# The down stage's last round in two parts, with four token tiles of the final norm between the second part's products

## The chip, the cores and the metric

The kernel runs on one core of a Trainium2 chip, as one launch. The metric is the device time of one execution in microseconds (us); lower is better. TensorE (PE) multiplies, VectorE (DVE), ScalarE (ACT) and GpSimd (POOL) do the rest, and SyncE (SP) issues the DMAs. Each engine runs its own instructions in program order; between engines, order comes from semaphore waits alone.

## What is computed

One layer of a streaming encoder for 1024 prompt tokens and 128 sample tokens (8 requests of 16), all in float32, width 1024:

```python
xp = half_ffn(xp, ...)            # f1:  x + 0.5 * ((silu(a) * b) @ w_down),  a, b = split(rmsnorm(x) @ w_up)
h  = rmsnorm(x);  x = x + W_out(gates * (sparse attention, matrix memory))
xp = half_ffn(xp, ...)            # f2
y  = rmsnorm(x) * norm_final      # the final norm
```

`w_up` is 1024 x 5632 and `w_down` 2816 x 1024. The outputs are y for all tokens, new keys and values, and the new memory states. The change touches both FFNs and the final norm; the middle of the layer is left as it is.

## The kernel before

`ffn` (from line 520) is built twice, as f1 and f2. The 1152 tokens are held transposed in `xT`, eight row blocks of 128 features by 1152 tokens, in two halves of 576. Each matrix product is done by a scheme of seven block products instead of eight: a weight tile of 256 columns is split into 2 x 2 blocks, the activations into 2 x 2 (feature halves and token halves), sums and differences are formed of both, and products 0 to 6 of each tile go through PSUM chains that yield four output blocks. Block 0 and 2 belong to the first token half, blocks 1 and 3 to the second. Each number is carried as a high and a low part, so a product of weights and activations is three matmuls (`product3`, lines 517 to 519) for each of two token quarters and each feature group.

The up stage has weight tiles 0 to 21, the down stage tiles 22 to 41 in five rounds of four tiles: four rounds over two groups of hidden features (12 matmuls a product) and the last one over three groups (18 matmuls a product). The hidden activations are packed by ScalarE and VectorE (`pack_hi`, `pack_lo`, after `combine`) into one of three staging buffers, stored to DRAM by SyncE, and loaded again as operands of the down rounds (`load_operand`).

The order is written out by hand. `AT` lists all products; `step(n, q)` is the place of product q of tile n in it. At each step TensorE waits for the low part of its weights (`lo_ok`) and for its PSUM bank (`free_bank`, line 1072), and does the product. ScalarE casts the weights of four products later (`split_hi`, line 751), GpSimd subtracts for the low part (line 869). VectorE first evicts the product just done (`accumulate`, lines 923 and 927: half of the chain is added to a block of `xT`), and then does the rest that tables place at this step: `pack_lo` (line 972) from `LO_AT`, `combine` (lines 960 to 968) from `COMB_AT`, weight terms (differences of weight blocks, line 890) from `TERMS_AT`, the residual (`ADD_AT`), and in f1 additions of squares (line 981). VectorE and ScalarE stay in this order whatever comes late.

Two lines decide which products depend on each other:

```python
CHAIN = (0, 1, 0, 2, 0, 2, 0)          # PSUM chain of products 0..6
def bank(n, q): return (n - 2 + CHAIN[q]) % 3
```

Products 0, 2, 4, 6 of a tile follow each other in one bank pair, 3 and 5 in another, 1 alone. Product q may begin only when the bank's former product has been evicted. In the order 0 to 6 there is always another product between two of the same bank.

The final norm (`FinalNorm`) comes after the last product and its eviction, for nine tiles of 128 tokens: `turn` (eight transposes on TensorE into a PSUM pair, line 482), `square` with the row's sum (ScalarE, 491), `inverse` (VectorE, 498 and 501), `root` (ScalarE, 505), `result` (VectorE, 511), and the store (SyncE, 474). Tiles 0 to 7 alternate between two PSUM pairs, tile 8 has a third. Turn t waits for result t − 2.

Of the kernel before, what the change touches and what calls it, by code (L numbers as in the profile page):

```python
# [24 lines left out]
P = 128  # L25
# [422 lines left out]
class FinalNorm:  # L448
# [12 lines left out]
    def pair(self, t):  # L461
        at = 4 if t == 8 else t % 2 * 2
        return self.ps[:, at:at + 2, :].rearrange("p b n -> p (b n)")
# [5 lines left out]
    def store(self, sp):  # L469
        for t in range(NT):  # L470
            sp.wait_ge(self.r_ok, t + 1)
            dst = self.out["y_prompt"][0, t * P:(t + 1) * P, :] if t < NTP else \
                self.out["y_sample"].rearrange("b q d -> (b q) d")
            sp.dma_start(dst, self.res[:, t]).then_inc(self.st, 16)
        sp.wait_ge(self.st, 16 * NT)

    def turn(self, pe, t):

        if 2 <= t < 8:
            pe.wait_ge(self.r_ok, t - 1)  # L480
# [26 lines left out]
    def result(self, dve, t):  # L507

        dve.wait_ge(self.root_ok, t + 1)
        dve.wait_ge(self.ld, 16)  # L510
        self.nc.vector.scalar_tensor_tensor(self.res[:, t], self.pair(t), self.K["root"][:, t:t + 1],  # L511
                                            self.gain[:], ALU.mult, ALU.mult).then_inc(self.r_ok, 1)
# [9 lines left out]
def ffn(nc, ctx, M, K, w_up, w_down, gain, xT, xT_at, places, h_dram, r_dram, tag, first, last_io=None):  # L522
# [9 lines left out]
    def step(n, q):  # L532
        return 8 * n + q if n < 2 else 16 + 7 * (n - 2) + q

    def slot_no(n, x):
        return 4 * n + x if n < 2 else 8 + 7 * (n - 2) + x
# [3 lines left out]

    SLOTS, STEPS = slot_no(UPS + DOWNS, 0), step(UPS + DOWNS, 0)
    U_SLOTS, U_STEPS = slot_no(UPS, 0), step(UPS, 0)
    AT = [(n, q) for n in range(UPS + DOWNS) for q in range(8 if n < 2 else 7)]
    OWNER = [(n, x) for n in range(UPS + DOWNS) for x in range(4 if n < 2 else 7)]
    FREED = {last_use(j - RING): j for j in range(RING, SLOTS)}
    TERMS_AT = {}
    for n in range(2, UPS + DOWNS):
        late = n == UPS
        for i, e in enumerate((-4, -4, 0 if late else -3, 1 if late else -1)):
            TERMS_AT.setdefault(step(n, 0) + e, []).append((n, i))  # L550
    HI_AT, LO_AT, COMB_AT = {}, {}, {}
    for g in range(NG):
        b = step(2, 0) - 7 if g == 0 else step(2 * g + 1, 0)
        for i, e in enumerate((8, 9, 10, 10, 11, 12, 13) if g == 0 else (2, 5, 6, 8, 9, 10, 11)):
            HI_AT.setdefault(b + e, []).append((g, i))
            LO_AT.setdefault(b + e + 1, []).append((g, i))
        COMB_AT[b + (9 if g == 0 else 7)] = (g, 0)
        COMB_AT[b + (11 if g == 0 else 8)] = (g, 1)
    SUM_HI_AT = {step(0, 7) + e: e for e in range(8)}
    RAW_AT = {step(n, 0) - (10 if n > 2 else 12): n for n in range(2, UPS + DOWNS)}  # L560
    assert len(RAW_AT) == UPS + DOWNS - 2
    SQ_STEP = (1, 4, 5, 6)
# [10 lines left out]
    for r in range(len(ROUNDS)):  # L573
        for q in range(7):
            at, size = OPERAND[r, q]
            s = max(u[2] for u in used if u[0] < at + size and at < u[0] + u[1])
            LOAD_AT.setdefault(max(s + 1, step(UPS + 4 * r - 4, 3 * q)) if r else s + 1, []).append((r, q, s + 1))
            used.append((at, size, step(UPS + 4 * r + 3, q)))
# [4 lines left out]
    with ExitStack() as mem, M.scope():  # L583
# [33 lines left out]
        if last_io is not None:  # L617
            z = FinalNorm(nc, sem, K, xT, *last_io, M.at("z_gain", [P, D_MODEL], K["acc_at"]),
                          M.at("z_junk", [P, D_MODEL], main_at), M.at("z_res", [P, NT, D_MODEL], main_at + 4 * D_MODEL), ps)
# [3 lines left out]
        def round_of(n):  # L623
            return ROUNDS[(n - UPS) // 4]
# [56 lines left out]
        def y_block(m, i):  # L681
            k, t = 2 * (m % 4) + (0, 1, 1, 0)[i], (0, 1, 0, 1)[i]
            return xT[:, k, t * HT:(t + 1) * HT]

        with nc.Block() as block:
            @block.sync
            def _(sp):
# [4 lines left out]
                def load_raw(n):  # L692
                    sp.wait_ge(lo_ok, slot_no(n - 1, 0))
# [44 lines left out]
                if last_io is not None:  # L738
                    z.load(sp)
# [3 lines left out]
            def _(act):  # L743
                def split_hi(j):
                    n, x = OWNER[j]
                    weights_in(act, n)
                    if n >= 2 and isinstance(SOURCE[x], int):
                        act.wait_ge(t_ok, 4 * (n - 2) + SOURCE[x] + 1)
# [61 lines left out]
                def square(e):  # L810
                    m, i = DOWNS - 4 + e // 4, e % 4
                    act.wait_ge(dn_ev, 7 * m + SQ_STEP[i] + 1)
                    if e >= 4:
                        act.wait_ge(sum_ok, e - 3)
                    else:
                        act.wait_ge(pl_ok, 7 * NG)
                    t = (0, 1, 0, 1)[i]
                    dst = K["acc"][:, t * HT:(t + 1) * HT] if e < 2 else sq[e % 2][:]
                    nc.scalar.activation(dst, y_block(m, i), ACT.Square).then_inc(sq_ok, 1)

                def rest(n, q):
                    s = step(n, q)
# [10 lines left out]
                    if last_io is None and n >= UPS + DOWNS - 4:  # L833
                        m = n - (UPS + DOWNS - 4)
                        if m and q == 0:
                            square(4 * m - 1)
                        if q in (2, 5, 6):
                            square(4 * m + (2, 5, 6).index(q))
# [21 lines left out]
                else:  # L860
                    for t in range(NT):
# [10 lines left out]
            def _(dve):  # L872
                v = nc.vector

                def weight_term(n, i):
                    weights_in(dve, n)
                    count = 4 * (n - 2) + i
                    if n > 2:
                        dve.wait_ge(lo_ok, slot_no(n - 1, TERM_SLOT[i]) + 1)
                    else:  # L880
                        dve.wait_ge(norm.sl_ok, 2)
                    if n == UPS and i >= 2:
# [3 lines left out]
                    if i in (1, 3):  # L886
                        dve.wait_ge(t_ok, count if i == 1 else count - 1)
                    a, b = ((part(n, 0, 1), part(n, 0, 0)), (part(n, 1, 1), term(n, 0)), (part(n, 1, 1), part(n, 0, 1)),
                            (part(n, 1, 0), term(n, 1)))[i]
# [18 lines left out]
                def accumulate(n, q):  # L908
                    m = n - UPS
                    i = (0, 0, 2, 1, 1, 2, 3)[q]  # L910
                    before = 7 * m + {1: 1, 4: 4, 5: 3}[q] if q in (1, 4, 5) else \
                        7 * (m - 4) + {0: 2, 2: 6, 3: 5, 6: 7}[q]
                    dve.wait_ge(mm_ok, step(n, q) + 1)
# [7 lines left out]
                    y = pairs(y_block(m, i))  # L921
                    if m < 4 and q in (0, 2, 3, 6):
                        v.tensor_scalar(y, chain(n, q), 0.5, None, ALU.mult).then_inc(dn_ev, 1)
                        return
                    if before > 0:
                        dve.wait_ge(dn_ev, before)
                    v.scalar_tensor_tensor(y, chain(n, q), 0.5, y, ALU.mult, ALU.add).then_inc(dn_ev, 1)  # L927
# [20 lines left out]
                def add_residual(e, t):  # L948
                    k, tok = 2 * (e % 4) + e // 4, norm.tok(t)
                    dve.wait_ge(y_in[e % 2], 16 * (e // 2 + 1))  # L950
                    dve.wait_ge(dn_ev, 7 * (4 + e + 1))
# [23 lines left out]
                def add_square(e):  # L975
                    t = (0, 1, 0, 1)[e % 4]
                    a = K["acc"][:, t * HT:(t + 1) * HT]
                    dve.wait_ge(sq_ok, e + 1)
                    if e >= 4:
                        dve.wait_ge(sum_ok, e - 3)  # L980
                    v.tensor_tensor(a, a, sq[e % 2][:], ALU.add).then_inc(sum_ok, 1)

                def rest(n, q):
                    s = step(n, q)
# [10 lines left out]
                    if last_io is None and n >= UPS + DOWNS - 4:  # L995
                        m = n - (UPS + DOWNS - 4)
                        if m and q < 2:
                            add_square(4 * m - 2 + q)
                        if m and q in (3, 6):
                            add_square(4 * m + (3, 6).index(q))  # L1000
# [32 lines left out]
                else:  # L1033
                    for t in range(NT):
# [4 lines left out]
            def _(pe):  # L1039
# [32 lines left out]
                def free_bank(n, q):  # L1072
                    m, adds = n - UPS, 3 * (n - 2)
                    if q == 0:
                        if n == 2:
                            pe.wait_ge(hm_ok, 3)
                        elif m <= 0:
                            pe.wait_ge(ad_ok, adds - 2)
                        else:
                            pe.wait_ge(dn_ev, 7 * (m - 1) + 2)  # L1080
                    if q == 1:
                        if n == 2:
                            pe.wait_ge(hm_ok, 4)
                        elif m <= 0:
                            pe.wait_ge(ad_ok, adds)
                        else:
                            pe.wait_ge(dn_ev, 7 * (m - 1) + 6)
                    if q == 3:
                        if m > 0:
                            pe.wait_ge(dn_ev, 7 * m)  # L1090
                        elif n % 2:
# [3 lines left out]
                    if q in (2, 4, 5, 6):  # L1095
                        if m >= 0:
                            pe.wait_ge(dn_ev, 7 * m + {2: 1, 4: 3, 5: 4, 6: 5}[q])
                        elif q == 6:
                            pe.wait_ge(ad_ok, adds + 2)
                        else:  # L1100
                            pe.wait_ge(cp_ok, adds + {2: 1, 4: 2, 5: 3}[q])
# [9 lines left out]
                def down(n, q):  # L1111
                    j, r = slot_no(n, q), (n - UPS) // 4
# [4 lines left out]
                    products(chain(n, q), j, lambda k: xd[r, q][:, k, 0], lambda k: xd[r, q][:, k, 1], len(ROUNDS[r]),  # L1117
                             q in (0, 1, 3))
# [12 lines left out]
                if last_io is not None:  # L1131
                    pe.wait_ge(dn_ev, 7 * DOWNS)
                    for t in range(NT):
# [2050 lines left out]
```

## Time and profile before

| | us |
|---|---|
| median of 3 runs | 2536.09 (2535.38 to 2536.65) |
| the profiled execution | 2538.52 |
| its span | 2536.7 |
| TensorE busy | 2469.3 |
| VectorE busy | 1651.9 |
| ScalarE busy | 992.5 |
| GpSimd busy | 914.1 |
| mean DMA rate | 142 GB/s |

All comes from one execution recorded by the hardware profiler. Busy time counts an engine's own instructions; TensorE's weight loads (PEld) run beside its matmuls. A matmul's end is modelled, so matmuls overlap in the record; the distance of their starts is the pace. "Idle before <- X" is the time an engine stood before an instruction, and X is what ended it, inferred from semaphores. f1 runs from about 80 us to 780 us, the middle until about 1750 us, f2 from there to the end. f1's down stage begins at about 528 us and f2's at about 2257 us; f2's last round of products ends at 2508.8 us.

### The profile page before, as it was taken

To read this page: it belongs to the slowest core of one execution; us is meant where nothing else is said; L and a number is where in the kernel's file an instruction comes from. 1 tells how busy PE (TensorE), PEld (TensorE's weight loads), DVE (VectorE), ACT (ScalarE), POOL (GpSimd) and SP (SyncE) were. 2 spreads that over 40 slices of the span, in tenths; PEclk is the share of its full clock that TensorE was granted. 3 is DMA by queue.
4 is the path that set the end of the run, shared out by engine and by line. 5 is a ranking of instruction groups with operands and counts; after the bars stand their busy time and mean duration, and the time that the engine had idled before them with its cause. 6 is when DMAs were issued, how large, how long until landed. Compare 5 with 4: busy or idle time off the path is not lost. (4 is left out here: it accounts for less than half of the span.)

```text
span 2536.7 us, 43065 instructions
## 1 busy us (share of the span) xinstructions
PE 2469.3 (97%) x16970; PEld 2399.8 (95%) x16970; DVE 1651.9 (65%) x2570; ACT 992.5 (39%) x1875; POOL 914.1 (36%) x739
## 2 busy tenths in 40 slices
PE   7999999999998999999998999998999999999997
PEld 7999999999997989999997888998999999999997
DVE  8776766667765328998645653424867576667864
ACT  5444444422233332212557864323434344432223
POOL 1444444444455111212224103421344444444442
PEclk8999999999998999999998999998999999999998
DMA  5343343497634212112334422333234334487751
GB/s 211 114 149 131 140 149 136 152 360 280 261 133 142 64 54 79 52 52 85 100 90 100 60 58 89 126 108 125 89 136 161 127 136 144 144 320 287 292 190 75
DMA packets 227304, 361.47 MB, mean 142 GB/s; under 512 B 39644, under 2 KB 174872, under 8 KB 226720
## 3 DMA queue, kind: packets, MB, share of 16 engines
q1 hardware_dynamic: 227104, 358.72, 41.0%
q8 instruction: 135, 2.21, 0.4%
q14 instruction: 65, 0.53, 0.1%
HBM read 231.21 MB, written 126.26 MB: 141 GB/s over the span
## 5 line engine op out<-in xcount | busy, mean ns | idle before, releaser
L517 PE MATMUL f1ps<-f1xs_lo,f1w_hi 128*128 128x288 f32 x1248 | 369.0, 296 | 3.7 <-DVE f1xs_lo L417 3.7
L517 PE MATMUL f2ps<-f2xs_lo,f2w_hi 128*128 128x288 f32 x1248 | 368.3, 295 | 3.7 <-DVE f2xs_lo L417 3.7
L519 PE MATMUL f1ps<-f1xs_hi,f1w_hi 128*128 128x288 f32 x1248 | 369.2, 296 | 0.0
L519 PE MATMUL f2ps<-f2xs_hi,f2w_hi 128*128 128x288 f32 x1248 | 368.7, 295 | 0.0
L518 PE MATMUL f1ps<-f1xs_hi,f1w_lo 128*128 128x288 f32 x1248 | 368.6, 295 | 0.0
L518 PE MATMUL f2ps<-f2xs_hi,f2w_lo 128*128 128x288 f32 x1248 | 368.1, 295 | 0.0
L517 PE MATMUL d_ps<-xn_lo,d_w_hi 128*128 128x384 f32 x864 | 298.5, 345 | 6.9 <-POOL xn_lo L297 5.3
L518 PE MATMUL d_ps<-xn_hi,d_w_lo 128*128 128x384 f32 x864 | 293.6, 340 | 0.0
L519 PE MATMUL d_ps<-xn_hi,d_w_hi 128*128 128x384 f32 x864 | 293.5, 340 | 0.0
L517 PEld LDWEIGHTS f1ps<-f1xs_lo,f1w_hi 128*128 128x128 f32 x1248 | 235.1, 188 | 5.1 <-POOL f1w_lo L869 4.1
L517 PEld LDWEIGHTS f2ps<-f2xs_lo,f2w_hi 128*128 128x128 f32 x1248 | 234.7, 188 | 4.7 <-issue 3.9
L518 PEld LDWEIGHTS f1ps<-f1xs_hi,f1w_lo 128*128 128x128 f32 x1248 | 235.1, 188 | 0.1
L519 PEld LDWEIGHTS f1ps<-f1xs_hi,f1w_hi 128*128 128x128 f32 x1248 | 235.2, 188 | 0.0
L519 PEld LDWEIGHTS f2ps<-f2xs_hi,f2w_hi 128*128 128x128 f32 x1248 | 234.8, 188 | 0.0
L518 PEld LDWEIGHTS f2ps<-f2xs_hi,f2w_lo 128*128 128x128 f32 x1248 | 234.7, 188 | 0.1
L1565 POOL TENSOR_TENSOR d_w_lo<-d_raw,d_w_hi 128x1024 fp32r<-128x1024 f32 x36 | 86.4, 2399 | 406.6 <-ACT d_w_hi L1430 406.6
L517 PE MATMUL f1ps<-f1xd,f1dw_hi 128*128 128x288 f32 x616 | 182.7, 297 | 3.4 <-issue 2.8
L517 PE MATMUL f2ps<-f2xd,f2dw_hi 128*128 128x288 f32 x616 | 183.1, 297 | 3.0 <-issue 2.8
L1859 DVE TENSOR_SCALAR_CACHE_REDUCE sel_hits<-DM,sel_cand 128x1024 uint8<-128x1024 f32 (+6 forms) x217 | 184.9, 917 | 1.1
L519 PE MATMUL f2ps<-f2xd,f2dw_hi 128*128 128x288 f32 x616 | 183.2, 297 | 0.0
L518 PE MATMUL f2ps<-f2xd,f2dw_lo 128*128 128x288 f32 x616 | 182.7, 297 | 0.0
L519 PE MATMUL f1ps<-f1xd,f1dw_hi 128*128 128x288 f32 x616 | 182.6, 296 | 0.0
(416 smaller groups left out, 6069.1 us busy)
## 6 DMA issues: line engine op xcount, KB each, us to landing
h_dram<-f1stg SPq DMA_DIRECT2D x77, 576.0 KB, 3.3
f1xd<-h_dram SPq DMA_DIRECT2D x77, 576.0 KB, 8.0
h_dram<-f2stg SPq DMA_DIRECT2D x77, 576.0 KB, 3.3
f2xd<-h_dram SPq DMA_DIRECT2D x77, 576.0 KB, 8.1
f1raw<-in_w_ffn_up SPq DMA_DIRECT2D x22, 1024.0 KB, 6.4
f2raw<-in_w_ffn_up SPq DMA_DIRECT2D x22, 1024.0 KB, 6.4
d_raw<-in_w_in SPq DMA_DIRECT2D x35, 512.0 KB, 5.1
p_dram<-stage SPq DMA_DIRECT2D x24, 576.0 KB, 3.4
```

The costliest lines, as they stand in the source:

```text
L517: nc.tensor.matmul(out, w_hi, x_lo, start=first, stop=False, skip_group_check=onto)
L518: nc.tensor.matmul(out, w_lo, x_hi, start=False, stop=False, skip_group_check=onto)
L519: return nc.tensor.matmul(out, w_hi, x_hi, start=False, stop=final, skip_group_check=onto)
L1565: nc.gpsimd.tensor_tensor(w_lo[:, n0 % 2], raw[:, n0 % 2], w_hi[:, n0 % 2].bitcast(F32), ALU.subtract).then_inc(lo_ok, 1)
L1859: v.tensor_scalar(hits[:, off:off + L], views[j], limit, None, ALU.is_ge, ALU.add, accum_out=cnt[:, j:j + 1]).then_inc(cnt_ok, 1)
```

## The change

- The last round's four tiles become eight. Tiles 38 to 41 do products 0, 1, 2, 3 and 5 and so finish blocks 0 and 2, the first 576 tokens. Tiles 42 to 45 do products 4 and 6, which add to blocks 1 and 3. This holds for f1 and f2.
- Product 2 of the first part is evicted into three blocks (2, 3, 1) instead of one, since the chain is cut there. Tiles 42 to 45 load their weights again (768 KB each) and form three weight terms each; tiles 38 to 41 form two instead of four.
- The second part's chains use banks 2 and 3 in turn, products 4 and 6 of a tile in the same bank.
- `free_bank` now finds the bank's former product in `AT` and waits for the last of its evictions.
- In f2, TensorE turns token tiles 0 to 3 ahead of the second, third, fifth and sixth product of the second part; ScalarE's square and root and VectorE's inverse follow at that step, the result at the next. Tiles 4 to 8 remain behind the last product and use four PSUM pairs. In f1 the squares are reordered to the blocks as they are finished.
- The packing and combining of the last up group (g = 10) moves: from steps 2, 5, 6, 8, 9, 10, 11 after the start of tile 21 to 8, 9, 10, 10, 11, 12, 13, the combines from 7 and 8 to 9 and 11; step 7 is the first product of the down stage.
- The final norm's gain is loaded after the last residual, its buffers lie elsewhere.

```diff
+    TILES = UPS + DOWNS + 4
+    SPLIT, LATE = TILES - 8, TILES - 4
+    PRODUCTS = [tuple(range(8))] * 2 + [tuple(range(7))] * (SPLIT - 2) + [(0, 1, 2, 3, 5)] * 4 + [(4, 6)] * 4
+        if n >= LATE:
+            places_of = (0, -4), (2, -4), (3, -3)
+        elif n >= SPLIT:
+            places_of = (0, -4), (1, -4)
+    ONTO = [((0,), (0,), (2,), (1,), (1,), (2,), (3,)), {0: (0,), 1: (0,), 2: (2, 3, 1), 3: (1,), 5: (2,)}, {4: (1,), 6: (3,)}]
...
-        for i, e in enumerate((8, 9, 10, 10, 11, 12, 13) if g == 0 else (2, 5, 6, 8, 9, 10, 11)):
+        late = g in (0, NG - 1)
+        for i, e in enumerate((8, 9, 10, 10, 11, 12, 13) if late else (2, 5, 6, 8, 9, 10, 11)):
...
+        COMB_AT[b + (9 if late else 7)] = (g, 0)
+        COMB_AT[b + (11 if late else 8)] = (g, 1)
...
+    TURN_AT = {step(LATE, x): t for t, x in enumerate((1, 2, 4, 5))} if last_io is not None else {}
...
         def bank(n, q):
+            if n >= LATE:
+                return 2 + n % 2
             return (n - 2 + CHAIN[q]) % 3
...
                 def free_bank(n, q):
+                    before = [x for x in AT[AT.index((2, 0)):AT.index((n, q))] if bank(*x) == bank(n, q)]
+                    if before and before[-1][0] >= UPS:
+                        pe.wait_ge(dn_ev, events_to(*before[-1]))
+                    elif n >= LATE:
+                        return
...
+                    if at(n, q) in TURN_AT:
+                        pe.wait_ge(dn_ev, events_to(LATE - 1, 5))
+                        z.turn(pe, TURN_AT[at(n, q)])
...
-                    for t in range(NT):
+                    for t in range(4, NT):
                         z.turn(pe, t)
```

In `FinalNorm` the pair of tile t becomes `2 * (t % 2 if t < 4 else t % 4)`, and turn t waits for result t − 2 up to tile 5, for the result of tile 3 at tiles 6 and 7, and for that of tile 4 at tile 8.

## Rows read from the trace of the kernel before

**Rows 1.** The page, busy time of each engine.
```profile
PE 2469.3 (97%) x16970; PEld 2399.8 (95%) x16970; DVE 1651.9 (65%) x2570; ACT 992.5 (39%) x1875; POOL 914.1 (36%) x739
```
**Rows 2.** Windows, last round: us, busy PE PEld DVE ACT POOL, PEclk, DMA, GB/s.
```profile
2475.00:2509.00 34.00, 33.80 (x256) 33.57 (x254) 14.53 (x20) 5.80 (x11) 12.44 (x11) 1.00 0.00 1
```
**Rows 3.** Timeline, TensorE, end of the last round: start, duration, instruction, idle before.
```profile
2508.52 0.29 PE L519 MATMUL f2ps<-f2xd,f2dw_hi 128*128 128x288 f32 x1
2509.66 1.97 PE L482 MATMUL f2ps<-ident_sb,xT 128*128 128x128 f32 x16 [0.85 <-DVE xT L927]
```
**Rows 4.** Timeline, VectorE, the last two evictions.
```profile
2506.47 0.76 DVE L927 SCALAR_TENSOR_TENSOR xT<-f2ps,xT 128x576 f32<-128x576 f32 x1 [1.62 <-PE f2ps L519]
2508.84 0.76 DVE L927 SCALAR_TENSOR_TENSOR xT<-f2ps,xT 128x576 f32<-128x576 f32 x1 [1.62 <-PE f2ps L519]
```
**Rows 5.** The chain that ended last, in the tail: start, us, what.
```profile
2509.66 1.10 PE f2ps L482 x8
2510.78 1.11 ACT z_junk L491 x2
...
2513.45 1.30 DVE z_res L511
...
2516.79 1.12 ACT z_junk L491 x2
...
2518.56 1.28 DVE z_res L511
...
2520.38 1.30 DVE z_res L511
...
2532.42 1.28 DVE z_res L511
```
**Rows 6.** Timeline, VectorE, f2's last round: an eviction and two weight terms.
```profile
2468.39 0.76 DVE L927 SCALAR_TENSOR_TENSOR xT<-f2ps,xT 128x576 f32<-128x576 f32 x1 [1.62 <-PE f2ps L519]
2469.07 0.55 DVE L890 TENSOR_TENSOR f2dts<-f2draw 128x384 f32<-128x384 f32 x1
2469.75 1.16 DVE L890 TENSOR_TENSOR f2dts<-f2draw,f2dts 128x384 f32<-128x384 f32 x1
```
**Rows 7.** Timeline, VectorE, f1's last round: additions of squares.
```profile
741.20 0.75 DVE L981 TENSOR_TENSOR acc<-acc,f1sq 128x576 f32<-128x576 f32 x1
...
747.04 1.57 DVE L981 TENSOR_TENSOR acc<-acc,f1sq 128x576 f32<-128x576 f32 x1
```
**Rows 8.** Timeline, VectorE, eviction of product 2 of tile 22.
```profile
2265.51 0.74 DVE L923 TENSOR_SCALAR xT<-f2ps 128x576 f32<-128x576 f32 x1
```
**Rows 9.** Timeline, TensorE, first down tile of f2.
```profile
2263.29 0.29 PE L519 MATMUL f2ps<-f2xd,f2dw_hi 128*128 128x288 f32 x1
2266.36 0.58 PE L517 MATMUL f2ps<-f2xd,f2dw_hi 128*128 128x288 f32 x1 [2.78 <-issue]
...
2272.01 0.44 PE L519 MATMUL f2ps<-f2xd,f2dw_hi 128*128 128x288 f32 x1
2272.26 0.38 PE L517 MATMUL f2ps<-f2xd,f2dw_hi 128*128 128x288 f32 x1
```
**Rows 10.** Windows of TensorE: us, busy, PEclk, DMA, GB/s.
```profile
806.00:808.00 2.00, 1.27 (x7) 1.00 1.20 299
...
2265.00:2270.00 5.00, 3.64 (x15) 0.56 1.03 422
```
**Rows 11.** DMA issues: out<-in, count, KB each, median us to landing.
```profile
h_dram<-f2stg SPq DMA_DIRECT2D x77, 576.0 KB, 3.3
...
f2draw<-in_w_ffn_down SPq DMA_DIRECT2D x4, 768.0 KB, 5.0
...
z_gain<-in_norm_final SPq DMA_DIRECT2D x1, 512.0 KB, 5.6
```
**Rows 12.** Waits (2255 to 2280; TensorE's 795 to 860): total, times, longest.
```profile
ACT f2stg L808 <- DMA h_dram<-f2stg: 3.3, 3, 2.4
...
PE d_ps L517 <- POOL xn_lo L297: 2.3, 5, 0.5
```

More of the change, by code:

```diff
@@ L530, in ffn @@
     CHAIN = (0, 1, 0, 2, 0, 2, 0)
[L532 to L536, printed above, removed]
+    TILES = UPS + DOWNS + 4
+    SPLIT, LATE = TILES - 8, TILES - 4
+    PRODUCTS = [tuple(range(8))] * 2 + [tuple(range(7))] * (SPLIT - 2) + [(0, 1, 2, 3, 5)] * 4 + [(4, 6)] * 4
+    STEP0 = [sum(len(x) for x in PRODUCTS[:n]) for n in range(TILES + 1)]
+    SLOT0 = [4 * n if n < 2 else STEP0[n] - 8 for n in range(TILES + 1)]
@@ L538, in last_use, with step, at, slot_no @@
+    def step(n, x):
+        return STEP0[n] + x
+    def at(n, q):
+        return STEP0[n] + PRODUCTS[n].index(q)
+    def slot_no(n, q):
+        return 4 * n + q if n < 2 else at(n, q) - 8
     def last_use(j):
         return 8 * (j // 4) + 4 + j % 4 if j < 8 else j + 8
[L541 to L544, printed above, removed]
+    SLOTS, STEPS = SLOT0[TILES], STEP0[TILES]
@@ L545, in ffn @@
+    U_SLOTS, U_STEPS = SLOT0[UPS], STEP0[UPS]
+    AT = [(n, q) for n in range(TILES) for q in PRODUCTS[n]]
+    OWNER = [(n, x) for n in range(TILES) for x in (range(4) if n < 2 else PRODUCTS[n])]
     FREED = {last_use(j - RING): j for j in range(RING, SLOTS)}
[L546 to L550, printed above, removed]
+    TERMS, TERMS_AT = [], {}
@@ L551, in ffn, with events_to, touched_before @@
+    EVENTS = [(n, q, i) for n in range(UPS, TILES) for q in PRODUCTS[n]
+              for i in ONTO[0 if n < SPLIT else 1 if n < LATE else 2][q]]
+    def events_to(n, q):
+        return 1 + max(x for x, e in enumerate(EVENTS) if e[:2] == (n, q))
+    def touched_before(x):
+        n, q, i = EVENTS[x]
+        return max([y + 1 for y in range(x) if (EVENTS[y][0] - n) % 4 == 0 and EVENTS[y][2] == i], default=0)
     HI_AT, LO_AT, COMB_AT = {}, {}, {}
@@ L623, in round_of @@
         def round_of(n):
-            return ROUNDS[(n - UPS) // 4]
+            return ROUNDS[min((n - UPS) // 4, len(ROUNDS) - 1)]
         def raw_of(n):
@@ L832, in rest @@
                         pack_hi(g, i)
[L833 to L838, printed above, removed]
+                    if last_io is None:
+                        for e in SQ_AT.get(s, ()):
+                            square(e)
+                    if s in TURN_AT:
+                        z.square(act, TURN_AT[s])
+                        z.root(act, TURN_AT[s])
                 norm.root(act)
@@ L920, in accumulate @@
                         dve.wait_ge(ra_ok, 2 * (m - 7))
[L921 to L927, printed above, removed]
+                    for x, (tile, product, i) in enumerate(EVENTS):
+                        if (tile, product) != (n, q):
+                            continue
+                        y = pairs(y_block(n, i))
+                        if touched_before(x) == 0:
+                            v.tensor_scalar(y, chain(n, q), 0.5, None, ALU.mult).then_inc(dn_ev, 1)
+                        else:
+                            dve.wait_ge(dn_ev, touched_before(x))
+                            v.scalar_tensor_tensor(y, chain(n, q), 0.5, y, ALU.mult, ALU.add).then_inc(dn_ev, 1)
                 def evict(n, q):
@@ L994, in rest @@
                         add_residual(*ADD_AT[s])
[L995 to L1000, printed above, removed]
+                    if last_io is None:
+                        for e in SUM_AT.get(s, ()):
+                            if e % 8:
+                                add_square(e)
+                    if s - 1 in TURN_AT:
+                        z.result(dve, TURN_AT[s - 1])
+                    if s in TURN_AT:
+                        z.inverse(dve, TURN_AT[s])
                 norm.inverse(dve)
@@ L1033, in _ @@
                 else:
-                    for t in range(NT):
+                    for t in range(4, NT):
                         z.inverse(dve, t)
@@ L1131, in _ @@
                 if last_io is not None:
-                    pe.wait_ge(dn_ev, 7 * DOWNS)
-                    for t in range(NT):
+                    pe.wait_ge(dn_ev, len(EVENTS))
+                    for t in range(4, NT):
                         z.turn(pe, t)
```

140 lines of the change are left out of this document (73 added, 67 removed).

## The prediction

> **What bounds the kernel now.** I read the page's busy times first: TensorE is busy 97% of the span [rows 1], so any time comes from its idle stretches, from work it does beside the products, or from the tail after its last product. The timelines come next, cut to the end. In the last down round TensorE is busy 33.80 of 34.00 us at full clock while the DMA stands still [rows 2], and VectorE evicts one product every 2.37 us [rows 4]: 18 matmuls each, so 0.132 us a matmul, and 12 matmuls or 1.58 us in the rounds of two groups. No product waits there, because the one ahead of it never touches the same bank. After the last eviction come nine token tiles of the final norm, in two bank pairs; the span ends at 2536.7 us, 27.1 us after that eviction's end at 2509.60. One more loss lies where the down stage begins: TensorE stands still for 2.78 us, and its matmuls then come 0.25 us apart until 2272.26 [rows 9].
>
> The trace is of f2, the second FFN; f1 runs the same code without the final norm and with squares instead.
>
> **The price of a product that follows its own bank.** The last eviction is the pattern: final matmul starts 2508.52 and lasts 0.29, VectorE starts 2508.84, takes 0.76, and TensorE starts again at 2509.66 [rows 3, 4]. Without a wait the next matmul would have started at 2508.65. So an adjacent dependence costs 1.0 us, and I take 1.05, since the first matmul after a wait is longer (0.58 against 0.44 in [rows 9]). Bounds: 0.85 (eviction and its two hand-overs, if the rest is hidden by the queue) and 1.3.
>
> **First part (tiles of products 0, 1, 2, 3, 5).** Products 3 and 5 share a bank and used to have product 4 between them. Now they are adjacent, and product 5 waits for the eviction of 3. That is four stalls in each FFN. Ahead of that eviction VectorE has product 2's evictions, now three instead of one: two at the spacing of back-to-back work, 0.68, and one of 0.76 [rows 4, 6], 2.1 us, which fits into 2.38. In f2 the two weight terms after product 1 take 0.55 and 1.16 [rows 6]; with the eviction that is 2.5 us, 0.15 over, still absorbed. In the fourth tile a third term (0.55 to 1.16 [rows 6], taken 0.7) follows the three evictions and delays the one of product 3 by 0.45. f2: 4 × 1.05 + 0.45 = 4.65 us. In f1 an addition of squares (0.75, or 1.57 beside a busy GpSimd [rows 7]) also stands behind the terms from the second tile on: 0.68 + 0.55 + 1.16 + 0.75 = 3.15 to 3.4, so the three evictions end about 0.7 after product 3 does. With 0.55 more in each of three tiles and 0.7 more in the last: 4.2 + 1.65 + 0.7 = 6.5 us.
>
> **Second part (tiles of products 4, 6).** Both use one bank, and only 6 continues the sum of 4, so each 6 waits for the eviction of 4. The first 4 uses the bank of the product just ahead of it too. f1: 5 stalls. VectorE there has, per tile, two evictions, three terms and two additions of squares, 6.5 us against 4.76 + 1.05 of TensorE, so it has no slack; 5 × 1.1 = 5.5 us. f1 loses 12.0 us together, and its own tail stays.
>
> f2: the first 4 stalls (1.05). Four turns of eight transposes go between the products: the first took 1.10 and two of them 1.97 [rows 3, 5], so 4 × 1.05, 4.2 us (3.9 to 4.4). Those ahead of a product 6 (two of them) cover the eviction. The two products 6 without one stall, and here the norm's small work gets into VectorE's queue. Behind its eviction at each turn stands the wait for ScalarE's square (1.11 [rows 5]), which itself stands behind a weight cast, which waits for a weight term on VectorE. I followed the queues from the end of the first product 6 (time 0): term and cast 2.2, square until 3.5, inverse until 3.85. The next product 4 ends at 3.5, its eviction therefore ends at 4.6, and product 6 starts at 4.65 (1.25 stalled). The result of tile 0 (1.30 [rows 5]) must wait for two more terms, 7.6; the third turn needs its bank pair and stalls 0.6. The fourth turn waits 0.2 for the result of tile 1, and the last product 6 stalls 0.85. Together 2.9 us of waits, with the first 4's 1.05 and the turns 8.2 us. The second reading of the weights costs nothing: its load takes 5.0 us [rows 11] and starts three products, 7.1 us, ahead of the terms; uncovered it would hold VectorE some 2 us a tile. The gain row likewise: 5.6 us [rows 11], some 15 us ahead. f2 loses 4.65 + 8.2 = 12.9 us before its tail.
>
> **The tail.** Now it holds five tiles with four bank pairs. From the last eviction's end: turn 1.10, square 1.11, inverse and root 0.65 (from 2516.79 + 1.12 to 2518.56), result 1.30 [rows 5]. Then each further tile costs what two results lie apart when their turn is ready, 20.38 − 18.56 = 1.82 [rows 5]: 4 × 1.82 = 7.3. After the last result 3.0 for the store (2536.7 − 2533.7, [rows 5]). Sum 14.5 us. The first root waits for its function table: 1.56 us lie between its square's end and the first result (2513.45 − 2511.89) where later tiles have 0.65 [rows 5]; that moves ahead, beside products. Gain 27.1 − 14.5 = 12.6 us; bounds 11.5 (one more wait for a turn) and 13.5. So f2's part nets 0.3 us slower: what the tail gives, the stalls and the turns take.
>
> **The last up group's packing moves about one down tile later.** In the old order VectorE does packing and combining in front of the eviction of product 2 of the first down tile: it starts at 2265.51 [rows 8], though product 3 behind it had ended at 2263.58 and so product 2 by 2262.0. TensorE waits for it, 2266.36 − 2263.29 less one matmul, 2.9 us, and then runs 24 matmuls at 0.25 instead of 0.13, 2.7 us more [rows 9]; the granted clock was 0.56 there, near its lower level of 1.2 GHz [rows 10]. This loss is 5.6 us per FFN. The new order frees this eviction and piles the packing up afterwards. In 11 products of 1.58 us, 17.4 us, VectorE has eleven evictions, seven packings, four combines and six terms, 28 pieces at about 0.7, 19.6 us. By my walk down the queues product 5 waits 0.4, product 6 waits 1.1 (behind a packing and two terms), product 1 of the next tile 1.5 (behind two packings, two combines, a term), product 2 of it 2.2, for ScalarE's packing must wait until a store has left its staging buffer: 3.3 us when the DMA is free [rows 11], up to 7 when full; ScalarE waited up to 2.4 for it before [rows 12]. Sum 5.2 us, and 1 us more for some matmuls at the lower clock. Per FFN that is 6.2 against the old 5.6, so +0.6; bounds −5.6 (all gone) and +5 (full DMA and a second clock drop).
>
> **Sum.** f1 12.0, f2 12.9 − 12.6 = 0.3, packing 2 × 0.6 = 1.2: +13.5 us. The profiled execution took 2538.5 us, its span 2536.7; by this it becomes 2552.0, span 2550.2. It lies 2.4 us over the median of the three runs, 2536.1; on that the forecast is 2549.6, taken as 2550.
>
> **Weighed against a rule.** In f1's second part TensorE would be busy 2.38 of 3.45 us, 69%, five times over. Rows show the clock at 1.00 in a stretch where it was busy 1.27 of 2.00 us, between waits of up to 0.5 us [rows 10, 12], and at half only after 2.78 us of standing [rows 9]. The Trainium skill's page "TensorE: Matmul & The Clock Gate", section "A second HAM failure mode: psum-queue depth-cycling", speaks against this change: matmul groups that pause briefly each time they cycle through PSUM banks can make the clock swing. By the row the sum stays +13.5; the rule's case is rival B, and nothing above uses it.
>
> **Rivals.**
> A, the forecast: stalls at 1 us, clock kept in the last round, 2550; own range 2543 to 2557. Chance 0.60.
> B, the clock falls in the last round. Place: the pauses of the parts, worst in f1's second. A matmul at the lower clock costs 0.12 more [rows 9], a product of 18 costs 2.1: over f1's eight late products 17 us, over half of them 8. 2558 to 2567, say 2562. For it: short repeated stalls that the old round lacks. Against: [rows 10]. 0.13.
> C, the other side: not slower. Place: the start of the down stage. If stores return in 3.3 us and no eviction queues, all 5.6 us in each FFN go: 12.3 − 11.2 = +1.1, 2537. It decides from about 4 us of gain per FFN (12.3 − 8 is inside the 5 us of no change), and each 0.2 us off the 16 stalls adds 3.2, to 2534. For it: evictions 0 to 3 are really freed. Against: VectorE's 20 us of work in 17.4. 0.15, of which a third lies below −0.2%.
> D, the change doesn't do what it says: the four early tiles come too late, because the weight loads of the second part or the norm's waits hold VectorE at each of the late tiles by some 2 us; 6 to 8 us more, 2557. 0.12.
>
> **Numbers.** 0.2% is 5 us, about what this kernel's measurement tells from none. Slower: A, B, D, and a little of C's upper end lies in no change: 0.82. Same 0.12, from C and the low end of A. Faster 0.06. The range 2539 to 2562 leaves out most of C and the upper part of B.
>
> **What would show it.** Product 5 of tiles 38 to 41 idle 0.85 us "<-DVE xT", in f1 up to 1.6; product 6 of the late tiles the same, five in f1. Span from last eviction to end near 14.5 us. Product 2 of the first down tile without a wait, and waits of 1 to 2 us in the tile after. Wrong if adjacent products wait under 0.5 us, if the down stage's start loses under 2 us, or if the granted clock falls in the last round.

## The result and the profile after

| | before | after |
|---|---|---|
| median | 2536.37 us (2535.38 to 2538.38, 4 runs) | 2563.84 us (2560.88 to 2565.94, 4 runs) |
| profiled execution / its span | 2538.52 / 2536.7 | 2560.88 / 2559.1 |

The ratio is 1.0106, 95% interval [1.0091, 1.0121]: the changed kernel is 1.1% slower. The direction was as forecast (2550 us), the size was not, and it lies 2 us above the range's upper end of 2562.

The page's busy times of the kernel after, to be held against [rows 1], come first. TensorE's work has not grown: it is busy 1.6 us less than before in a span 22.4 us longer, so its added time is standing. VectorE's has grown by 7.4 us.

```profile
PE 2467.7 (96%) x16970; PEld 2395.3 (94%) x16970; DVE 1659.3 (65%) x2594; ACT 990.4 (39%) x1875; POOL 905.6 (35%) x739
```

To find where, I cut the two traces at marks that both have: the last up product's multiply on VectorE, the eviction of product 0 of tile 24 (two tiles into the down stage), the start of the last eviction, and the end of the span.

| us, from the timelines | before f1 | after f1 | before f2 | after f2 |
|---|---|---|---|---|
| start: last multiply to product 0 of tile 24 | 29.2 | 35.2 | 29.6 | 36.1 |
| rest: from there to the last eviction | 221.9 | 233.5 | 221.9 | 234.7 |
| tail: last eviction's end to the span's end | | | 27.1 | 14.5 |

The last round and the tail are as forecast: +11.6 and +12.8 us in the rest (forecast 12.0 and 12.9), 14.5 us of tail (forecast 14.5). The start costs 6.0 and 6.5 us more; forecast was 0.6.

**The last round.** VectorE's timeline in the first part of f2 (start, duration, instruction, idle before). The eviction after three in a row is product 3's, the next one product 5's. Their distance is 3.52 us, where undisturbed products lie 2.39 apart: a stall of 1.13.

```profile
2472.00 2.07 DVE L970 SCALAR_TENSOR_TENSOR xT<-f2ps,xT 128x576 f32<-128x576 f32 x3
2474.32 0.76 DVE L970 SCALAR_TENSOR_TENSOR xT<-f2ps,xT 128x576 f32<-128x576 f32 x1 [0.24 <-PE f2ps L519]
2477.84 0.76 DVE L970 SCALAR_TENSOR_TENSOR xT<-f2ps,xT 128x576 f32<-128x576 f32 x1 [2.76 <-PE f2ps L519]
```

The same place in f1, where an addition of squares stands ahead of the three evictions. Four evictions run together without a gap, so product 3's comes late and TensorE waits 1.47 us before 755.12.

```profile
751.37 0.74 DVE L1024 TENSOR_TENSOR acc<-acc,f1sq 128x576 f32<-128x576 f32 x1
752.04 2.93 DVE L970 SCALAR_TENSOR_TENSOR xT<-f1ps,xT 128x576 f32<-128x576 f32 x4
```
```profile
755.12 0.37 PE L517 MATMUL f1ps<-f1xd,f1dw_hi 128*128 128x288 f32 x1 [1.47 <-DVE xT L970]
```

The windows of the two last rounds show what became of the clock (us, busy PE PEld DVE ACT POOL with counts, PEclk, DMA, GB/s): TensorE pauses in 13 to 16% of the time, in pauses of 0.9 to 1.5 us, and the granted clock stays at 1.00.

```profile
740.00:760.00 20.00, 17.06 (x128) 16.86 (x128) 11.33 (x15) 4.83 (x9) 7.52 (x7) 1.00 0.14 41
760.00:790.00 30.00, 25.29 (x184) 24.28 (x184) 18.71 (x30) 9.43 (x17) 9.41 (x9) 1.00 0.25 79
```
```profile
2500.00:2545.00 45.00, 39.30 (x291) 37.64 (x290) 24.99 (x42) 11.88 (x24) 11.43 (x11) 1.00 0.31 112
```

The tail, the chain that ended last (start, us, what): the first result begins 0.65 us after its square's end, where [rows 5] had 1.56, so the function table's wait is out of the tail as forecast. The five results lie 1.81 apart.

```profile
2544.64 1.10 PE f2ps L482 x8
2545.74 0.02 issue
2545.76 1.12 ACT z_junk L491 x2
...
2547.53 1.28 DVE z_res L511
...
2549.34 1.28 DVE z_res L511
...
2554.78 1.28 DVE z_res L511
```

**The start of the down stage.** Here is the difference to the forecast. First the waits of the kernel after in f2, 2273 to 2312 us (engine, line, waited for what: us in total, times, longest). Follow the wait back: product 2 of tile 23 waits 5.7 us for an eviction (L967); VectorE waits 3.9 us for ScalarE's packing (L845); and ScalarE waits up to 6.7 us for a store to leave its staging buffer (the first line). Before, the line of that last wait read 3.3 us in 3 waits, the longest 2.4 [rows 12].

```profile
ACT f2stg L845 <- DMA h_dram<-f2stg: 11.9, 4, 6.7
...
PE f2ps L517 <- DVE xT L967: 5.7, 1, 5.7
DVE xT L967 <- PE f2ps L519: 5.7, 5, 2.0
...
DVE f2stg L1015 <- ACT f2stg L845: 3.9, 1, 3.9
PE f2ps L517 <- issue: 1.8, 2, 1.4
PE f2ps L517 <- DVE xT L970: 1.5, 1, 1.5
```

The timelines put them in order. SyncE's queue: ahead of the store issued at 2285.27 stand two loads of the next round's operands (L746, 576 KB each) and one of weights.

```profile
2283.42 1.27 SPq L746 DMA_DIRECT2D f2xd<-h_dram  x2
2284.73 0.49 SPq L736 DMA_DIRECT2D f2draw<-in_w_ffn_down  x1
2285.27 0.51 SPq L760 DMA_DIRECT2D h_dram<-f2stg  x1
```

The times from issue to landing of the seven stores between 2275 and 2300 us are spread as follows; the median over all 77 of this kernel is 3.3.

```profile
DMA to landing us min/median/max: 3.2/6.6/8.8
```

A slow return is not new at this place. In the kernel before, the six stores between 2258 and 2275 us were no quicker:

```profile
DMA to landing us min/median/max: 5.3/7.3/8.3
```

What the new order took away is the room for it. There are three staging buffers, so each packing takes the buffer of the third one before it. In the old order (steps 2, 5, 6, 8, 9, 10, 11) the last four packings come 6, 4, 4 and 3 steps after the one whose buffer they take; in the new (8, 9, 10, 10, 11, 12, 13) 2, 2, 2 and 3. ScalarE now waits at all four: 3.1 and 1.8 us for stores that took 3.7 and 3.2, then 6.7 for one that took 8.5, then 0.4.

ScalarE stands for that buffer from 2287.24 (2293.90 − 6.66) and gets it 8.6 us after the store's issue. Queued behind the packing on ScalarE is a weight cast.

```profile
2293.90 0.68 ACT L845 ACTIVATE f2stg<-f2g 128x576 fp32r<-128x576 f32 x1 [6.66 <-DMA h_dram<-f2stg]
2294.49 0.40 ACT L788 ACTIVATE f2dw_hi<-f2dts 128x256 fp32r<-128x256 f32 x1
```

VectorE stands at the low half of the same packing; the eviction that frees product 2's bank is two places behind it.

```profile
2294.61 0.76 DVE L1015 TENSOR_TENSOR f2stg<-f2g,f2stg 128x576 fp32r<-128x576 f32 x1 [3.94 <-ACT f2stg L845]
2295.29 0.95 DVE L934 TENSOR_TENSOR f2dts<-f2draw,f2dts 128x256 f32<-128x256 f32 x1
2296.16 0.74 DVE L967 TENSOR_SCALAR xT<-f2ps 128x576 f32<-128x576 f32 x1
```

TensorE starts again 0.89 us later, after 5.74 us, and its matmuls come 0.24 us apart until 2301.75. The windows show the granted clock: 1.00 in the first, 0.71 in the second, which holds most of the standing, 0.61 in the third, toward the lower level of 1.2 GHz.

```profile
2297.05 0.58 PE L517 MATMUL f2ps<-f2xd,f2dw_hi 128*128 128x288 f32 x1 [5.74 <-DVE xT L967]
2297.43 0.44 PE L518 MATMUL f2ps<-f2xd,f2dw_lo 128*128 128x288 f32 x1
2297.67 0.44 PE L519 MATMUL f2ps<-f2xd,f2dw_hi 128*128 128x288 f32 x1
```
```profile
2288.00:2293.00 5.00, 1.83 (x12) 1.62 (x12) 2.67 (x4) 0.00 (x0) 0.39 (x1) 1.00 1.00 313
2293.00:2298.00 5.00, 0.95 (x4) 0.98 (x5) 3.39 (x5) 2.28 (x5) 2.64 (x3) 0.71 0.88 333
2298.00:2303.00 5.00, 5.00 (x26) 5.00 (x25) 1.41 (x3) 0.66 (x2) 1.01 (x2) 0.61 0.96 294
```

Waits of 5.7 + 1.8 + 1.5 us and 20 matmuls 0.11 late each (2.1) make 11.1 us, against 2.8 + 2.7 before: 5.6 of the 6.5 that the start grew. The idle time in front of a matmul is less than the wait costs, and there are now four waits for one. Counted from start to start of the 184 matmuls (those 0.16 to 0.32 us apart as slow ones, more than that as standing, each above the pace of 0.132), it is 10.0 us of standing against 3.2 and 2.3 us of slow matmuls against 2.6 in f2, 9.7 against 3.6 and 1.6 against 1.8 in f1. All the growth is standing; the lower clock is in both kernels, and has no part in it. In f1 the longest wait is 5.5 us and ends on product 2's weights (the cast queued behind the same waiting packing) instead of its bank.

### The profile page after: what moved, and what is told of

The parts are those of the page before. It is cut to its first block and busy times, and to the rows that moved or that the text cites. A ratio compares the mean times of both kernels' runs of the same rounds, so it can differ in the third digit from the quotient of the medians.

```text
span 2559.1 us, 43105 instructions
## 1 busy us (share of the span) xinstructions
PE 2467.7 (96%) x16970; PEld 2395.3 (94%) x16970; DVE 1659.3 (65%) x2594; ACT 990.4 (39%) x1875; POOL 905.6 (35%) x739
## 5 line engine op out<-in xcount | busy, mean ns | idle before, releaser
L518 PEld LDWEIGHTS f2ps<-f2xs_hi,f2w_lo 128*128 128x128 f32 x1248 | 234.7, 188 | 0.1
```

Of the source, the lines that this page charges most:

```text
L518: nc.tensor.matmul(out, w_lo, x_hi, start=False, stop=False, skip_group_check=onto)
```

## The experiments

Theory: the late packing costs about 6 us per FFN, because ScalarE now waits for staging buffers whose stores come back late behind the next round's loads; the stalls and turns of the last round cost what was forecast. Rivals: the packing's cost is VectorE's order of work alone; it is of the memory layout or of some other part of the change; or the parts don't add up. Each run below was timed against the kernel before on the same chip; its median there was 2536.75 to 2537.38 us. "Start", "rest" and "tail" are the segments of the table above, f1 and f2.

**pack_back**: the change without its packing edit.

```diff
-        late = g in (0, NG - 1)
+        late = g == 0
```

> The changed kernel with the packing and combining of the last up group put back to its old steps; all else as changed. Theory: the later packing alone costs 6.0 us in f1 and 6.5 us in f2 over the old start of the down stage (time from the last up product's multiply to the eviction of product 0 of tile 24: 35.2 and 36.1 us against 29.2 and 29.6), so both return to 29.2 to 29.6 and the median falls from 2563.8 by 12 to 15 us, to 2549 to 2552. Rival: the start is slower for another part of the change (bank waits, order of the DMA issues), then it stays at 35 to 36 us and 2563.

Measured 2550.17 us (2548.24 to 2552.62, 5 runs), ratio 1.0053 [1.0040, 1.0067]. Start 29.3 and 29.2, rest 233.6 and 234.7, tail 14.5. So without the packing edit the change costs 13.4 us by the ratio, with it 26.9.

**pack_only**: the kernel before with the packing edit alone (the same line, the other way).

> The kernel before with only the later packing and combining of the last up group, in both FFNs. Theory: 2536.4 + 12.5, 2548 to 2552, with ScalarE waiting over 5 us for a staging buffer's store at the start of each down stage and TensorE standing 5 us behind it. Rival: without the split it makes no difference, 2535 to 2539.

Measured 2550.22 us (2548.10 to 2550.53, 5 runs), ratio 1.0051 [1.0038, 1.0063]. Start 35.7 and 35.7, rest 221.9 twice, tail 27.1. Alone it costs 12.9 us; 12.9 and 13.4 add up to the 26.9 within their intervals. The packing edit is half of the loss, and neither half needs the other.

**loads_later**: the change, with the loads of the down stage's second round issued at steps 10 to 25 of the stage instead of 0 to 18, each 7 to 10 steps later. (What was written down ahead of mid_loads and loads_only calls the same edit 10 to 15 steps later, in the last up group.)

```diff
-            LOAD_AT.setdefault(max(s + 1, step(UPS + 4 * r - 4, 3 * q)) if r else s + 1, []).append((r, q, s + 1))
+            first_at = step(UPS, 10 + 5 * q // 2) if r == 1 else step(UPS + 4 * r - 4, 3 * q)
+            LOAD_AT.setdefault(max(s + 1, first_at) if r else s + 1, []).append((r, q, s + 1))
```

> The changed kernel with the loads of the second round's operands issued from step 10 after the start of tile 22 on, one every two or three steps, instead of from step 0 every three. Theory: the store that ScalarE waits 6.7 us for is slow because those loads are ahead of it in the DMA queues; the wait falls under 4 us and the time by 4 to 8 us, 2556 to 2560. Rival: it is VectorE's load of work alone (19.6 us of pieces in 17.4), and the start stays at 35 to 36 us, 2562 to 2565.

Measured 2551.91 us (2546.66 to 2556.51, 4 runs), ratio 1.0057 [1.0042, 1.0073]: a gain of 12 us where 4 to 8 were expected, the same as pack_back, while all packing stays late. Start 29.5 twice, rest as in the change. Its waits in f2's start, 2265 to 2304 us, answer to those above: the longest for a store is 2.7 and TensorE's longest 2.5.

```profile
ACT f2stg L846 <- DMA h_dram<-f2stg: 7.6, 4, 2.7
...
PE f2ps L517 <- DVE xT L968: 2.5, 1, 2.5
PE f2ps L517 <- issue: 1.4, 1, 1.4
```

The DMA issues from 2270 to 2305 us (tile, engine, count, KB each, median us from issue to landing) say why; the first two rows are of the change, the last of this kernel. The store takes 6.6 us in the one and 4.0 in the other.

```profile
f2xd<-h_dram SPq DMA_DIRECT2D x10, 576.0 KB, 8.2
h_dram<-f2stg SPq DMA_DIRECT2D x7, 576.0 KB, 6.6
```
```profile
h_dram<-f2stg SPq DMA_DIRECT2D x7, 576.0 KB, 4.0
```

And the clock, in the windows over the wait and behind it, stayed at 1.00:

```profile
2280.00:2285.00 5.00, 2.17 (x15) 1.72 (x13) 4.34 (x7) 2.29 (x5) 2.08 (x3) 1.00 0.94 381
2285.00:2290.00 5.00, 4.95 (x37) 4.98 (x38) 3.71 (x5) 0.84 (x2) 2.86 (x4) 1.00 0.82 277
```

What the late packing costs over the old order is thus what its stores have to wait behind loads. It takes both, the short room between packings and the slow return: the old order with the same loads starts in 29.2 and 29.6 us, and the late order with those loads moved back in 29.5, against 35.2 and 36.1 for both together.

**order_swap**: the first part's tiles do product 3 before product 2, so that product 2 stands between 3 and 5, which share a bank.

```diff
-[(0, 1, 2, 3, 5)] * 4
+[(0, 1, 3, 2, 5)] * 4
```

> The changed kernel with products 2 and 3 of the first part's tiles exchanged (order 0, 1, 3, 2, 5), so that product 2 stands between 3 and 5, which share a bank. Theory: the four stalls in each FFN go, with what stood ahead of product 3's eviction: 4.65 us in f2 and 6.5 us in f1, so 11 us, 2551 to 2555, and no wait over 0.3 us before product 5. Rival: VectorE's three evictions and squares are what holds TensorE in f1, and the waits move to the product after; then 6 to 8 us, 2556 to 2558.

Measured 2553.77 us (2552.89 to 2557.58, 5 runs), ratio 1.0069 [1.0056, 1.0082]. Rest 229.0 and 230.5, 4.5 us less in f1 and 4.2 in f2. No wait over 0.2 us is left in the first part, but the rival is right in part: a wait has moved on. The first product of the second part, whose bank is that of the product just ahead of it, now waits 2.13 us in f1 and 1.46 in f2 (0.90 in both before the swap), since VectorE has two weight terms, and in f1 an addition of squares, ahead of that eviction.

```profile
767.70 0.37 PE L517 MATMUL f1ps<-f1xd,f1dw_hi 128*128 128x288 f32 x1 [2.13 <-issue]
```

So 4.5 and 4.2 are what the swap gives back net. What the first part's four stalls cost is read better further down, from all_three against two_banks, where that bank is free: 5.3 us in f1 and 4.8 in f2.

**two_banks**: in the second part products 4 and 6 of a tile use different banks; 4 is evicted into blocks 1 and 3, and 6 starts its own sum.

```diff
-{4: (1,), 6: (3,)}]
+{4: (1, 3), 6: (3,)}]
...
-                return 2 + n % 2
+                return 3 if q == 4 else 2
...
-                             q in (0, 1, 3) or n >= LATE and q == 4)
+                             q in (0, 1, 3) or n >= LATE)
```

> The changed kernel with products 4 and 6 of the second part in a bank pair each, product 4 evicted into two blocks instead of one, so no product follows its own bank there. Theory: five stalls of 1.1 us go in f1 and three (1.05, 1.25, 0.85) in f2, 8.6 us, 2554 to 2557; the eight added evictions (0.68 each) stay hidden. Rival: they lengthen VectorE's queue before the norm's results and the turns wait instead, so f2 gains nothing and the total is 5 us, 2558 to 2560.

Measured 2552.29 us (2551.64 to 2553.84, 5 runs), ratio 1.0063 [1.0050, 1.0075]. Rest 227.8 and 232.0, 5.7 and 2.7 us less, 8.4 together where 8.6 were expected; the median fell by more, 11.5. In f2 part of the gain goes into turns that now wait for a result (`z_res`, 1.9 us in two waits, 0.5 before).

**all_three**: pack_back, order_swap and two_banks together.

> Packing back, products 2 and 3 exchanged, and products 4 and 6 in two bank pairs, together in the changed kernel. Theory: the down stage's start is as before, f1 gains and loses nothing (within 1 us), and f2 keeps only the turns (4.2 us) and some waits of the norm (1 to 2 us) against a tail 12.6 us shorter: 2537.4 - 7, 2529 to 2532. Rival: the parts hide each other (one VectorE queue), and f1 keeps 3 us or more, 2534 to 2537.

Measured 2531.00 us (2529.56 to 2535.75, 11 runs), ratio 0.9980 [0.9971, 0.9989]. Start 29.0 and 29.2, rest 222.5 and 227.2, tail 14.5. f1's rest is 0.6 above the kernel before: all but that of its loss was these two sorts of stall. Against two_banks the rest is 5.3 and 4.8 us shorter, the first part's share. What is left in f2 is the turns, with one wait of 1.4 us for a result (`z_res`) among them.

**no_turns**: all_three with all nine norm tiles behind the last product and the old two bank pairs. This asks what the early norm is worth by itself.

```diff
...
-    TURN_AT = {step(LATE, x): t for t, x in enumerate((1, 2, 4, 5))} if last_io is not None else {}
+    TURN_AT = {step(LATE, x): t for t, x in enumerate(())}
...
```

> The same kernel, but with all nine tiles of the final norm behind the last product, as before the change. Theory: the last round in two parts costs nothing by itself once no product follows its own bank, 2536 to 2539, and the difference to the kernel with the turns is 12.6 - 4.2 less 1 to 2, some 7 us. Rival: reading the weights twice and the added evictions cost by themselves, 2541 or more.

Measured 2538.49 us as the median of 11 runs (lowest 2534.20; one run of 8661 us lies outside all others; without it the median is 2537.97), ratio 1.0000 [0.9991, 1.0009]. Rest in f2 222.0, tail 25.9. The turns among the products cost 5.2 us and save 11.4 of the tail: 6.2 net in the profiled executions, 5 by the ratios. The tail of 25.9 is 1.2 shorter than before with the same nine tiles behind the products: some of its turns ran at the higher clock, 1.11 us in place of 1.98.

**pack_mid**: all_three, with the last group's packing spread a little: steps 2, 5, 6, 9, 10, 11, 12, combines at 8 and 9.

```diff
-        for i, e in enumerate((8, 9, 10, 10, 11, 12, 13) if late else (2, 5, 6, 8, 9, 10, 11)):
+        for i, e in enumerate((8, 9, 10, 10, 11, 12, 13) if late else (2, 5, 6, 9, 10, 11, 12) if g == NG - 1 else (2, 5, 6, 8, 9, 10, 11)):
...
-        COMB_AT[b + (9 if late else 7)] = (g, 0)
-        COMB_AT[b + (11 if late else 8)] = (g, 1)
+        COMB_AT[b + (9 if late else 8 if g == NG - 1 else 7)] = (g, 0)
+        COMB_AT[b + (11 if late else 9 if g == NG - 1 else 8)] = (g, 1)
```

> The same kernel as all_three, with the last up group's packing only partly later: the first three pieces at their old steps (2, 5, 6), the others one step later (9 to 12), the combines at 8 and 9. Theory: TensorE's wait of 2.9 us at product 4 of the first down tile and the lower clock after it (5.6 us per FFN) come from the combine and the packing ahead of product 2's eviction; with the combine one step later the wait falls under 1 us and the clock stays, 8 to 10 us less than all_three, 2520 to 2523. Rival: the same work then stands before a later eviction, as with the fully later packing, and it gains under 3 us.

Measured 2529.22 us (2527.47 to 2529.74, 6 runs), ratio 0.9967 [0.9955, 0.9979]. A miss: I had expected most of the old loss at the start to go, and the start is only 0.3 and 0.7 us shorter, 28.7 and 28.5. The granted clock did stay at 1.00 through both starts, but TensorE's wait of 2.8 us came back as four waits of 0.7 to 1.5. The next two runs ask why.

**mid_loads**: pack_mid with the second round's loads issued later, as in loads_later.

> pack_mid (packing order put back with the last group's steps a little apart, the first part's pieces in the order 0, 1, 3, 2, 5, two banks for the second part) with one edit more: the loads of the next round's operands are issued later in a tile, from a step 10 to 15 later in its last up group, as in loads_later. Theory 1 (what is left of the down stage's late start is the store of a staging buffer that comes back behind those loads on the queue): the stretch from the last up product to the eviction of product 0 of tile 24, 28.7 and 28.5 us in pack_mid, falls by another 1 to 3 us per FFN, and the time is 2523 to 2528 us. Rival (VectorE's and ScalarE's own work sets that stretch, the queue no longer): the stretch stays within 0.5 us and the time within 2528 to 2531 us. Rival 2 (the loads come too late and the last round's first products wait for them): rest of the stage longer by 1 us or more, time over 2531 us.

Measured 2527.77 us (2525.66 to 2529.59, 5 runs), ratio 0.9965 [0.9951, 0.9978]. Start 27.9 and 28.0, 0.8 and 0.5 us less than pack_mid's in the profiled executions; the ratios of the two can't be told apart. The rival is nearer than the theory: the queue had little left to give. The windows from 2261 us on show VectorE busy 4.97 of 5 us while TensorE has 3.54, and the DMA then down to 0.55.

```profile
2261.00:2266.00 5.00, 3.54 (x27) 3.34 (x26) 4.97 (x6) 1.41 (x4) 4.14 (x4) 1.00 0.95 385
2266.00:2271.00 5.00, 3.51 (x25) 3.10 (x24) 4.87 (x8) 2.15 (x5) 2.90 (x3) 1.00 0.55 163
```

**loads_only**: the kernel before with later loads alone.

> The kernel before with one edit alone: the loads of the next round's operands are issued 10 to 15 steps later in the last up group. Theory 1 (as the prediction read the kernel before: the 2.9 us that product 2 of tile 22 waits comes from the order of VectorE's work ahead of its eviction): no change, the start stays at 29.2 and 29.6 us, time 2535 to 2538 us. Rival (there too a store comes back late behind the loads): the start falls by 1 to 4 us per FFN, time 2527 to 2534 us.

Measured 2536.37 us (2533.76 to 2539.89, 11 runs), ratio 0.9999 [0.9991, 1.0008]: no change, and TensorE's wait of 2.8 us is there as before. The old order's loss is set by VectorE's work in front of one eviction, as the prediction read it; only the late order's growth is set by the DMA queue. The start itself is 28.6 and 28.5 us, 0.6 and 1.1 less than in the kernel before. In this execution the granted clock stayed at 1.00 in both FFNs, and 24 matmuls behind the wait ran at full pace, but TensorE then stood at the product after:

```profile
2268.97 0.37 PE L517 MATMUL f2ps<-f2xd,f2dw_hi 128*128 128x288 f32 x1 [1.44 <-issue]
```

So more than half of the 2.7 us that the prediction put on the slow matmuls is a wait when they are fast. What ends that second wait the trace doesn't name.

mid_loads and pack_mid are the fastest kernels of this case, 0.35% and 0.33% below the kernel before.

## Why the prediction missed its size

- **Adjacent products on one bank, 1.05 us each: right.** TensorE is idle 0.90 to 1.03 us at such a stall, and from start to start it costs 1.05 to 1.19; where squares stand ahead, in f1's second and third tile, the idle time is 1.47. The first part's four cost 5.3 and 4.8 us (forecast 6.5 and 4.65). f1's was too high because the fourth tile was to wait 2.3 us and waited 1.03. The second part's five in f1 cost 5.7 (forecast 5.5).
- **Whole last round, 12.0 and 12.9: right**, 11.6 and 12.8. f2's hand walk down the queues (turns 4.2 and the waits around them) held in sum, in part by luck. Counted from start to start, the seven stalls took 7.7 us and the four turns 3.7 (forecast 4.2); the waits of 0.6 and 0.2 for the norm's results did not come; and 1.3 us lie in the first, slower matmuls behind each stop, which the forecast left out. Pairs of weight terms there took from 1.01 to 1.83 us on VectorE, which [rows 6] let expect.
- **Tail 14.5: right to 0.1 us.** no_turns gives the trade by itself: 11.4 saved, 5.2 paid. The old tail isn't a constant: it was 27.1 us before and 25.9 in no_turns.
- **Rival B (the clock falls in the last round): refuted**; all its windows stand at 1.00. By that, the rule which the prediction weighed from the Trainium skill ("TensorE: Matmul & The Clock Gate", "A second HAM failure mode: psum-queue depth-cycling") didn't come true here, with pauses of 0.9 to 1.5 us between products of 2.4. The row that spoke against B was weaker than it looked: it is 2 us long, and in the same trace the window from 815 to 820 us stands at 0.67, behind a pause of 1.45. Rival D (loads and norm hold VectorE there): refuted, since the rest is as forecast. Rival C (the start is freed): refuted; it went the other way.
- **"The last up group's packing moves": this step failed.** It was put at 6.2 us per FFN against an old 5.6, so +0.6, 1.2 in all, with a bound of +5; measured is +6.0 and +6.5, 12.5 in all, above even the bound. The place was named (product 2 of the tile after, behind a packing that waits for a store), but its wait was 2.2 us in the walk and 5.7 in the trace. The three waits before it were put at 3.0 us and measure 3.3. The mistake is in the store's return: I took 3.3 us for it, "when the DMA is free", though [rows 11] give that as the median of the whole kernel, and kept 7 for the bound. At this place the DMA isn't free. The six stores there took 5.3 to 8.3 us in the kernel before already, where it could be read, and the one that counts, behind two 576 KB loads and one of weights, took 8.5. The old order hid such returns behind its 3 to 6 steps from a buffer's packing to its next; the new one leaves 2 or 3. A second, smaller miss: the slow matmuls took 2.3 us in f2 and 1.6 in f1, where the new order's sum had 1. They took 2.6 and 1.8 in the old order too, and runs in which the clock stayed up start only 0.6 to 1.1 us sooner, so the clock is no part of the growth.

The sum with this one term put right is 13.5 + 11.3 = 24.8 us, 2561; by the ratio it was +26.9 (23 to 31), in the profiled executions +22.4. The segments of the table above add up to +24.3; what the change doesn't touch (before f1's down stage and between f1 and f2) took 1.9 us less in that execution. The rest of the difference is which executions were profiled: before, one 2.2 us over the median, and after, the fastest of four, 3.0 under it. Why executions of one kernel differ by that much stays open.

## What to carry to other kernels

When a step is moved, follow its DMA too: count the steps from each use of a buffer to the next, and price the buffer's return by the stores of that place (5.3 to 8.3 us here, in the trace of the kernel before), not by the median over the kernel (3.3). Slow matmuls behind a wait are not a loss in full: ask what TensorE would wait for next if they were fast. If two products share a bank, put one between them that doesn't: both sorts of stall here went away by such a choice, at the price of one eviction more per tile in one of them. Moving a tail's work among the products pays (6.2 us net here), if the split that makes it possible is kept free of stalls of its own.

## What the runs showed that was not expected

The granted clock doesn't follow the length of one pause alone. A pause of 2.8 us at the down stage's start was followed by a window at 0.50 in the kernel before and by windows at 1.00 in loads_only, with the same instructions; in loads_later a longest pause of 2.5 left it at 1.00 as well. The first row is of before, the second of loads_only, each the window right behind that pause's.

```profile
2267.00:2272.00 5.00, 5.00 (x22) 5.00 (x22) 4.72 (x7) 1.82 (x4) 2.31 (x3) 0.50 1.03 407
```
```profile
2265.00:2270.00 5.00, 3.56 (x28) 3.35 (x27) 4.76 (x7) 2.80 (x6) 3.24 (x4) 1.00 0.88 293
```

It differs even within one execution. In pack_back both FFNs stand 2.77 us at that place, with the same instructions; the windows just behind are these, f1's first. The two starts took 29.3 and 29.2 us, so the fall cost nothing that shows there.

```profile
538.00:543.00 5.00, 3.47 (x26) 3.26 (x26) 4.65 (x7) 1.99 (x4) 2.63 (x3) 1.00 1.03 416
2278.00:2283.00 5.00, 5.00 (x30) 5.00 (x30) 4.73 (x8) 2.09 (x4) 2.51 (x3) 0.73 1.03 418
```

The Trainium skill says of a kernel's start ("TensorE: Matmul & The Clock Gate", "Part 1: The HAM clock gate (the "warmup" mystery)") that how many matmuls of one kernel run slow varies from run to run. That is another place, and no kernel here was profiled twice; the two FFNs of pack_back agree with it in kind.
